# A two-layer transformer kernel: the second attention written out between the weight chunks of its query groups and of the output projection

## Chip, cores and metric

One core of one Trainium2 chip. The metric is the device time of one execution in microseconds (us), lower is better; the kernel before has a median of 2048.22 us in 3 runs (2047.43 to 2049.34).

## What is computed

Two layers on a sequence of 256 tokens with 2048 features, all in float32. Layer 0 has a latent attention (MLA), layer 1 a windowed attention with sinks; each is followed by a feed-forward block with a width-3 convolution. The change lies in layer 1's attention: 32 query heads of 64 features, 4 key/value heads, a window of 128 keys, a bias by distance, and a sink logit per head that enters the softmax's maximum and its sum.

```python
def _swa_sinks(h, rel_bias, w_qkv, b_qkv, sinks, w_o, b_o):
    qkv = h @ w_qkv + b_qkv
    q = qkv[..., :nq] ... * SWA_HEAD_DIM ** -0.5     # 32 heads x 64
    ...
    m, l, acc = _banded_stats(q, k, v, bias, SWA_WINDOW - 1)   # blocks of 128 queries, own and previous block's keys
    m2 = jnp.maximum(m, sink)
    a = jnp.exp(m - m2)
    den = l * a + jnp.exp(sink - m2)
    o = acc * (a / den)[..., None]
    return o.reshape(bsz, t, nq) @ w_o + b_o
```

## The kernel before, in words

**Weights as a stream.** Activations lie transposed in SBUF, features on the 128 partitions and 256 tokens along the row. All weights come as one stream of 682 chunks (128 × 1024 floats, 512 KB), in the order in which they are used; `PH` gives each phase its chunks and its groups of 4 output tiles: a_in, a_q, a_kv, a_out, f0_in, f0_out, b_in (40 chunks, 5 groups), b_out (32 chunks, 4 groups), f1_in, f1_out. Four slots hold chunks in flight. SyncE loads a chunk into `raw` once the slot's last split is done; ScalarE (ACT, L735) rounds it to fp32r as `w_hi`, once TensorE has used the chunk four before; VectorE (DVE, L999) subtracts to get the remainder `w_lo`; TensorE (PE) multiplies. Operands are split in the same way into a high and a low half that lie side by side. For each 128 × 128 block of weights PE makes two matmuls: w_hi with high and low half together (512 columns, L387) and w_lo with the high half (256 columns, L390). One output tile so fills a whole PSUM bank: columns 0 to 255 and 256 to 511 have to be added, and a group of 4 tiles takes 4 of the 8 banks. `token_chunk` (L416 to L418) makes three matmuls of 256 columns instead, with the operand as weights; it gives keys and values by token.

**Leaving PSUM.** `b_half` on ACT (L744) copies the second half of a group's banks to `half_b`; DVE then adds it to the first half (`sum_banks`, L1075, or `add_residual`, L1256 and L1258, for sums into `h`), and frees the banks.

**Second attention.** b_in's first group gives keys and values, the other four the queries (`q_win`). After the last b_in chunk come 16 units of two heads. For each: PE makes the scores (`scores_b`, L676, two heads on the two halves of the rows); DVE adds the bias and takes the maxima (L1189, L1196); ACT takes the exponentials with their sums (L842) and those of the sinks (L846); DVE adds the sinks' to the sums and scales (L1209, L1211, L1218); PE transposes (L551); ACT copies the transposed to SBUF (L854); PE multiplies by the values (`values_b`, L684, L685); ACT and DVE split the result into `op_att` (L966, L1373). GpSimd (POOL) stages keys, values and biases and ACT the queries (L952), because the units run in hardware loops, with fixed places for the operands. Two units are in flight, in eight banks. Only two chunks of b_out are put between the last units (`early_chunk`); else no chunk is multiplied in this stretch. Then b_out goes on group by group, and `residual` adds it to `h`.

All engines run in program order; semaphores between them (`chunk_used`, `lo_ready`, `scores_done`, `maxima_done`, `probs_ready`, `probs_t_copied`, `outputs_done`, `outputs_hi`, `outputs_lo`, `banks_free`) set the order of work.

Of the kernel before, what the change touches and what calls it, by code (L numbers as in the profile page):

```python
# [13 lines left out]
P = 128  # L14
# [56 lines left out]
UNITS_A, UNITS_B = HEADS_A // 2, HEADS_B // 2  # L71

# [77 lines left out]
def build(nc, xt, positions, rel_bias, params, weights, swa_b_v, swa_sinks, c_ident, c_rot, c_invf, c_mask,  # L150
# [37 lines left out]
    sink_exps = new("sink_exps", [P, 2, 4])  # L188
# [58 lines left out]
    q_win = place("q_win", [P, KT, T], F32, rg)  # L249
# [5 lines left out]
    with ctx:  # L255
# [13 lines left out]
        win_bias_in = sem("win_bias_in")  # L269
# [37 lines left out]
        k_both_ready = sem("k_both_ready")  # L307
        nsink_ready = sem("nsink_ready")
        bias_staged = sem("bias_staged")
        q_placed = sem("q_placed")  # L310
# [70 lines left out]
        def _(pe):  # L381
# [252 lines left out]
            def plain_groups(g, n, op, per):  # L634

                for gi in range(2):
                    b0 = banks_of(g + gi)
                    for c in range(per):
                        w_chunk(n + (gi * per + c), op, 2 * c, c == 0, c == per - 1, b0).then_inc(chunk_used, 1)

# [25 lines left out]
            repeat(pe, 0, 2, lambda i: plain_groups(Lin(ph.g0 + 1, 2, i), Lin(ph.c0 + 8, 16, i), op_in, 8))  # L666

            def scores_b(u, bank):
                p = u.mod(2)
                if u.i is None and u.c < 2:  # L670
                    pe.wait_ge(k_both_ready, u.c + 1)
                pe.wait_ge(q_placed, (u + 1).v)
                for hh in range(2):
                    r = slice(64 * hh, 64 * hh + 64)
                    for q0, keys, o in ((0, P, 0), (P, T, P)):
                        z = mm(ps[:, bank + hh, o:o + keys], st_qb[r, p, q0:q0 + P], st_k[r, p, 0:keys],  # L676
                               start=True, stop=True)
                return z

            def values_b(u, bank):  # L680
                p = u.mod(2)
                for hh in range(2):
                    r = slice(64 * hh, 64 * hh + 64)
                    mm(ps[r, bank, 0:T], st_vb[:, p, 0, :], probs_t[p][:, hh, 0:T], start=True, stop=False)  # L684
                    z = mm(ps[r, bank, P:T], st_vb[:, p, 1, :], probs_t[p][:, hh, T:384], start=False, stop=True)  # L685
                return z

            attention(UNITS_A, UNITS_B, scores_b, values_b, attention_banks(PH["b_out"]), ph,
                      early_chunk(PH["b_out"], 2, UNITS_A))
            groups(PH["b_out"], op_att, KT, att_wait(UNITS_A + UNITS_B), start=EARLY)  # L690
# [33 lines left out]
        def _(act):  # L724
# [12 lines left out]
            def b_half(g, last_chunk, tiles=4, bias=None):  # L737

                act.wait_ge(chunk_used, (last_chunk + 1).v)
                if g.i is not None or g.c >= 1:  # L740
                    act.wait_ge(banks_free, g.v)
                b0 = 4 * g.mod(2)
                if bias is None:
                    f(half_b[:, 0:tiles, :], ps[:, b0:b0 + tiles, T:2 * T], ACT.Copy).then_inc(b_copied, 1)  # L744
                    return
                for j in range(tiles):
                    z = f(half_b[:, j, :], ps[:, b0 + j, T:2 * T], ACT.Identity, bias=bias(j))
                z.then_inc(b_copied, 1)
# [86 lines left out]
            def attention(u0, units, banks, sinks, out_high, place_q=None):  # L835
                def exps(u):
# [7 lines left out]
                    if sinks:  # L844
                        for hh in range(2):
                            z = f(sink_exps[:, p, 2 * hh:2 * hh + 2], neg_max[:, p, 2 * hh:2 * hh + 2], ACT.Exp,  # L846
                                  bias=sinkc[:, sl(u.times(2) + hh, 1)])
# [13 lines left out]
                def step(u, ahead=True):  # L861
                    if u.i is not None or u.c >= 2:
                        o_high(u - 2)
                    if ahead:
                        exps(u + 1)
                    if place_q and (u.i is not None or u.c < units - 3):
                        place_q(u + 3)
                    pt_copy(u)
                exps(Lin(0))
                if place_q:  # L870
                    place_q(Lin(2))
# [10 lines left out]
            attention(0, UNITS_A, banks, False,  # L882
# [6 lines left out]
            def residual(ph, kts, k0, bias=None):  # L889
# [3 lines left out]
                def body(i, t=0):  # L893
                    for j in range(2 * per):
                        split(Lin(ph.c0 + AHEAD + j + 2 * per * t, 2 * per, i))
                        gi, at = divmod(j, per)
                        if at == per - 5:
                            b_half(Lin(ph.g0 + gi + 2 * t, 2, i), Lin(ph.c0 + (gi + 1) * per - 1 + 2 * per * t, 2 * per, i),
                                   bias=bias and (lambda m: par[:, sl(Lin(bias + 4 * gi + m, 8, i), 1)]))
                        if at == per - 3 and k0 is not None:  # L900
                            op_high(Lin(k0 + gi, 2, i), op_in[:, sl(Lin(4 * gi, 8, i), 4), 0, :])
                if k0 is not None:
# [35 lines left out]
            def b_body(i):  # L938
                for j in range(16):
                    split(Lin(ph.c0 + AHEAD + SLOTS + j, 16, i))  # L940
                    if j in (7, 15):
                        b_half(Lin(ph.g0 + (j + 1) // 8, 2, i), Lin(ph.c0 + 8 + j, 16, i))
            repeat(act, 0, 2, b_body)
            banks = attention_banks(PH["b_out"])

            def place_q(u):

                if u.i is not None or u.c >= 2:
                    act.wait_ge(scores_done, (u + UNITS_A - 1).v)
# [39 lines left out]
        def _(dve):  # L989
# [144 lines left out]
            def q_group(k, cols, last=False):  # L1134
                dve.wait_ge(b_copied, (k + (ph.g0 + 1)).v)
# [510 lines left out]
```

## Time and profile before

| | |
|---|---|
| median of 3 runs | 2048.22 us |
| profiled execution | 2049.23 us, its span 2047.4 us, mean granted TensorE clock 0.994 |
| busy: PE, PEld, DVE, ACT, POOL | 97%, 86%, 71%, 50%, 9% of the span |
| HBM read | 362.85 MB |

The span runs from the first to the last instruction. Matmuls are pipelined: the time of one holds its way through the array, so that two which follow each other overlap in the rows, and the distance of their starts (the pitch) is what one costs.

### The profile page before, as it was taken

The page shows a single profiled execution, that of the slowest core. Times are in us where ns is not written, and L with a number is a line of the kernel's source. Part 1 is how long each engine was busy: PE and PEld are TensorE (multiplying, and loading weights), DVE is VectorE, ACT ScalarE, POOL GpSimd, SP SyncE. Part 2 cuts the span into 40 slices and gives each one's busy share as a digit, 9 for nine tenths or more (in the row PEclk, how much of TensorE's full clock was granted, in tenths as well). Part 3 has the DMA queues.
Part 4 walks back from the last instruction along what each step waited for, and adds up shares of the span by engine and source line. Part 5 has one row for each costly group of instructions (what it writes and reads, how often), then busy time and mean ns, then how long its engine had stood idle before and what let it go on. Part 6 is the DMA issues. An engine that isn't in the chain of part 4 may idle for free.

```text
span 2047.4 us, 33736 instructions
## 1 busy us (share of the span) xinstructions
PE 1988.8 (97%) x11624; PEld 1750.6 (86%) x11624; DVE 1452.0 (71%) x1988; ACT 1014.0 (50%) x1227; POOL 194.4 (9%) x258
## 2 busy tenths in 40 slices
PE   5999999999999999999999789999999999999998
PEld 5789888888888888888898568888888888888887
DVE  7776588778778877654566767887887787755554
ACT  4456445555554554434344775555545555534343
POOL 4202130000000000110120222200000000001110
PEclk9999999999999999999999899999999999999999
DMA  6458455555555555556576215555555655555553
GB/s 209 135 188 205 152 187 175 190 201 184 192 192 180 184 195 196 187 182 202 188 248 211 88 51 187 188 182 198 185 177 190 202 184 192 191 192 187 193 187 113
DMA packets 103009, 372.25 MB, mean 182 GB/s; under 512 B 11451, under 2 KB 12028, under 8 KB 102940
## 3 DMA queue, kind: packets, MB, share of 16 engines
q1 hardware_dynamic: 100316, 360.45, 52.6%
q0 software_dynamic: 2624, 10.83, 2.1%
q8 instruction: 50, 0.82, 0.2%
q14 instruction: 19, 0.16, 0.0%
HBM read 362.85 MB, written 8.39 MB: 181 GB/s over the span
## 4 chain that ended last, share of the span: by engine, by line
PE 90%; DVE 3%; issue 1%; ACT 0%; DVEq 0%; ACTq 0%
PE ps L387 57%; PE ps L390 30%; DVE scores_sb L1189 1%; DVE probs L1218 1%; PE ps L418 1%; PE ps L417 1%; PE ps L416 1%; PE ps L551 0%; PE ps L598 0%; DVE w_lo L999 0%; PE ps L589 0%; PE ps L591 0%; DVE q_nope L1137 0%; PE ps L676 0%; PE ps L600 0%
## 5 line engine op out<-in xcount | busy, mean ns | idle before, releaser
L999 DVE TENSOR_TENSOR w_lo<-raw,w_hi 128x1024 fp32r<-128x1024 f32 (+1 forms) x682 | 830.6, 1232 | 516.3 <-ACT w_hi L735 493.6
L387 PE MATMUL ps<-op_in,w_hi 128*128 128x512 f32 x3248 | 1120.0, 392 | 20.5 <-DVE w_lo L999 18.9
L735 ACT ACTIVATE w_hi<-raw 128x1024 fp32r<-128x1024 f32 (+1 forms) x682 | 715.5, 1055 | 830.0 <-PE ps L390 673.1
L390 PE MATMUL ps<-op_in,w_lo 128*128 128x256 f32 x3248 | 884.3, 282 | 0.0
L387 PEld LDWEIGHTS ps<-op_in,w_hi 128*128 128x128 f32 x3248 | 598.6, 188 | 135.2 <-issue 18.6
L390 PEld LDWEIGHTS ps<-op_in,w_lo 128*128 128x128 f32 x3248 | 615.8, 190 | 17.0
L387 PE MATMUL ps<-op_ffn,w_hi 128*128 128x512 f32 x1408 | 486.2, 390 | 0.0
L390 PE MATMUL ps<-op_ffn,w_lo 128*128 128x256 f32 x1408 | 391.7, 282 | 0.0
L387 PEld LDWEIGHTS ps<-op_ffn,w_hi 128*128 128x128 f32 x1408 | 262.2, 188 | 53.0
L390 PEld LDWEIGHTS ps<-op_ffn,w_lo 128*128 128x128 f32 x1408 | 266.0, 189 | 2.7
L1408 POOL TENSOR_TENSOR cg<-h 128x1024 f32 (+1 forms) x15 | 43.5, 2898 | 1499.9 <-DVE h L1258 1499.9
L387 PE MATMUL ps<-op_att,w_hi 128*128 128x512 f32 x512 | 176.3, 392 | 2.5 <-issue 2.5
L390 PE MATMUL ps<-op_att,w_lo 128*128 128x256 f32 x512 | 139.0, 282 | 0.0
L387 PEld LDWEIGHTS ps<-op_att,w_hi 128*128 128x128 f32 x512 | 94.0, 188 | 20.8 <-issue 3.2
L390 PEld LDWEIGHTS ps<-op_att,w_lo 128*128 128x128 f32 x512 | 96.7, 189 | 2.6
L1298 DVE SCALAR_TENSOR_TENSOR cv<-up,par,cv 128x256 f32<-128x256 f32 x176 | 73.6, 480 | 6.5 <-DVE cv L1293 3.3
L1298 DVE SCALAR_TENSOR_TENSOR cg<-up,par,cg 128x256 f32<-128x256 f32 x176 | 73.6, 480 | 6.6 <-DVE cg L1293 3.4
L744 ACT ACTIVATE half_b<-ps 128x1024 f32<-128x1024 f32 (+2 forms) x72 | 68.1, 946 | 10.0 <-PE ps L387 10.0
L753 ACT ACTIVATE op_ffn<-cv 128x1024 f32 x22 | 23.4, 1066 | 93.0 <-DVE cv L1323 93.0
L1411 POOL TENSOR_TENSOR sqa<-sqa,cg 128x256 f32<-128x256 f32 x60 | 62.8, 1046 | 4.7
L387 PE MATMUL ps<-op_lat,w_hi 128*128 128x512 f32 x160 | 57.4, 403 | 0.0
L1081 DVE TENSOR_TENSOR up<-up,inv_rms 128x1024 f32<-128x1024 f32 x44 | 53.9, 1225 | 1.5
(178 smaller groups left out, 1233.6 us busy)
## 6 DMA issues: line engine op xcount, KB each, us to landing
raw<-weights SPq DMA_DIRECT2D x666, 512.0 KB, 3.8
raw<-weights SPq DMA_DIRECT2D x16, 384.0 KB, 3.0
bias_rows<-brow POOLq DMA_DIRECT2D x1, 6144.0 KB, 36.2
win_bias<-bias_rows POOLq DMA_DIRECT2D x4, 1024.0 KB, 8.8
h<-xt SPq DMA_DIRECT2D x4, 512.0 KB, 7.0
y<-yt SPq DMA_DIRECT2D x4, 512.0 KB, 3.6
par<-params SPq DMA_DIRECT2D x1, 352.0 KB, 9.7
mask<-c_mask POOLq DMA_DIRECT2D x1, 192.0 KB, 3.7
```

What stands on the lines that cost most here:

```text
L387: return mm(ps[:, bank, 0:2 * T], whi, op, start=start, stop=stop)
L390: return mm(ps[:, bank, 0:T], wlo, op[:, 0, :], start=False, stop=False)
L416: mm(o, hi, wcols(w_hi[s], k), start=first and k == 0, stop=False)
L417: mm(o, hi, wcols(w_lo[s], k), start=False, stop=False)
L735: f(w_hi[s][:, 0:cols], raw[s][:, 0:cols], ACT.Copy).then_inc(hi_ready, 1)
L744: f(half_b[:, 0:tiles, :], ps[:, b0:b0 + tiles, T:2 * T], ACT.Copy).then_inc(b_copied, 1)
L753: f(dst, cv[:, :, :], ACT.Copy).then_inc(operand_hi, 1)
L999: v.tensor_tensor(w_lo[s][:, 0:cols], raw[s][:, 0:cols], w_hi[s][:, 0:cols].bitcast(F32), ALU.subtract).then_inc(lo_ready, 1)
L1081: return v.tensor_tensor(dst, dst, spread(r[:, :], tiles), ALU.mult)
L1298: z = v.scalar_tensor_tensor(dst[:, m, :], up[:, m, tap:T + tap], col(tile0 + (w + tap * CT + m)), dst[:, m, :], ALU.mult, ALU.add)
L1408: done(g_.tensor_tensor(tmp, src, src, ALU.mult))
L1411: z = g_.tensor_tensor(acc[:, :], acc[:, :], tmp[:, j, :], ALU.add)
```

## The change

The second attention is written out, one unit after the other with constants, in between the chunks.

- On PE, chunks of the query groups 2 to 4 and 16 chunks of b_out (tiles 0 to 7; their order in the stream is `OUT_EARLY`) stand between the steps: chunk, transposes of u, chunk, values of u, scores of u+2. There is one set of score banks (0, 1) and one of transposes and values (2, 3).
- These 48 chunks and the first query group are "narrow": three matmuls of 256 columns (w_hi·high, w_lo·high, w_hi·low) that sum in place, two tiles to a bank, so that a group needs two banks and no second half. (32 chunks of queries, 16 of b_out.)
- DVE: `queries` makes a group's queries from the two banks; `q_win` holds two groups. The sink is written as one more column of the scores' rows and goes through the exponential and its sum; the addition of `sink_exps` and its two exponentials go.
- Nothing is staged: GpSimd's copies and ACT's `place_q` go.
- `b_half` goes from all residuals (a_out, f0_out, b_out, f1_out): DVE adds both halves straight from PSUM. b_out's bias is added there.

```diff
+OUT_EARLY = [(0, c) for c in range(6)] + [(1, c) for c in range(6)] + [(0, 6), (0, 7), (1, 6), (1, 7)]
+Q0 = PH["b_in"].c0 + 16
...
+            def narrow_chunk(n, op, kt0, first, last, bank):
+
+                s = n % SLOTS
+                pe.wait_ge(lo_ready, n + 1)
+                for j in range(4):
+                    o = ps[:, bank + j // 2, j % 2 * T:(j % 2 + 1) * T]
+                    for k in range(2):
+                        w = slice(k * COLS + j * P, k * COLS + (j + 1) * P)
+                        mm(o, w_hi[s][:, w], op[:, kt0 + k, 0, :], start=first and k == 0 and j % 2 == 0, stop=False)
+                        mm(o, w_lo[s][:, w], op[:, kt0 + k, 0, :], start=False, stop=False)
+                        z = mm(o, w_hi[s][:, w], op[:, kt0 + k, 1, :], start=False, stop=last and k == 1 and j % 2 == 1)
+                z.then_inc(chunk_used, 1)
...
+            def scores_b_of(u):
+
+                if u == 0:
+                    pe.wait_ge(k_both_ready, KV_B)
+                if u % 4 == 0:
+                    pe.wait_ge(q_win_ready, u // 4 + 1)
+                if u >= 1:
+                    pe.wait_ge(maxima_done, UNITS_A + u)
...
+            def turn_p_b(u):
+
+                pe.wait_ge(probs_ready, UNITS_A + u + 1)
+                if u >= 1:
+                    pe.wait_ge(outputs_lo, UNITS_A + u)
...
+            for u in range(UNITS_B):
+                chunk(4 + 2 * u)
+                turn_p_b(u)
+                chunk(5 + 2 * u)
+                values_b_of(u)
+                if u + 2 < UNITS_B:
+                    scores_b_of(u + 2)
...
+            for u in range(UNITS_B):
+                split(Lin(Q0 + 7 + 2 * u))
+                if u >= 1:
+                    o_high_b(u - 1)
+                if u + 1 < UNITS_B:
+                    exps_b(u + 1)
+                pt_copy_b(u)
+                split(Lin(Q0 + 8 + 2 * u))
...
-                v.tensor_tensor(hh, hh, half_b[:, :, :], ALU.add).then_inc(banks_free, 1)
+                v.tensor_tensor(hh, hh, ps[:, b0:b0 + 4, T:2 * T], ALU.add).then_inc(banks_free, 1)
...
+            for u in range(UNITS_B):
+                if u + 1 < UNITS_B:
+                    maxes_b(u + 1)
+                split(Lin(Q0 + 7 + 2 * u))
+                if u >= 1:
+                    low_b(u - 1)
+                if u in (2, 6, 10):
+                    queries(PH["b_in"].g0 + 2 + u // 4, Q0 + 7 + 2 * (u - 2))
+                if u + 1 < UNITS_B:
+                    normal_b(u + 1)
+                split(Lin(Q0 + 8 + 2 * u))
```

The second of these loops is ACT's, the third DVE's. How the instructions stand, PE first. Before, in the loop of the attention (scores of a unit, transposes, values of the unit before, nothing else):

```order
L676 MATMUL ps<-st_k,st_qb 128x128 [waits q_placed]
L676 MATMUL ps<-st_k,st_qb 128x256
L676 MATMUL ps<-st_k,st_qb 128x128
L676 MATMUL ps<-st_k,st_qb 128x256
L551 MATMUL ps<-ident,probs_81 128x128 [waits probs_t_copied,probs_ready]
L551 MATMUL ps<-ident,probs_81 128x128 x5
L559 REGISTER_ALU [waits values_staged,probs_t_copied]
L684 MATMUL ps<-probs_t_84,st_vb 64x256 [waits outputs_lo]
L685 MATMUL ps<-probs_t_84,st_vb 64x128
```

After the change, a late unit (L728 transposes, L740 values, L717 scores, L679 to L681 a narrow chunk, 24 matmuls of which three stand here):

```order
L728 MATMUL ps<-ident,probs_b_117 128x128 [waits outputs_lo,probs_ready]
L728 MATMUL ps<-ident,probs_b_117 128x128 x5
L679 MATMUL ps<-op_att,w_hi_56 128x256 [waits lo_ready,outputs_lo]
L680 MATMUL ps<-op_att,w_lo_60 128x256
L681 MATMUL ps<-op_att,w_hi_56 128x256
...
L740 MATMUL ps<-probs_tb_119,cv 64x256 [waits probs_t_copied]
L740 MATMUL ps<-probs_tb_119,cv 64x256
L740 MATMUL ps<-probs_tb_119,cv 64x128 x2
L717 MATMUL ps<-k_both,q_win 128x128 [waits maxima_done]
L717 MATMUL ps<-k_both,q_win 128x128
L717 MATMUL ps<-k_both,q_win 128x256 x2
L679 MATMUL ps<-op_att,w_hi_53 128x256 [waits lo_ready,outputs_lo,banks_free]
```

A chunk now stands on either side of the transposes, and these wait for `outputs_lo` of the unit before as well. DVE before, from a unit's negative maxima to the low half of an older unit's output:

```order
L1196 SCALAR_TENSOR_TENSOR neg_max<-ri,nsink 128x4
L1209 TENSOR_TENSOR exp_sums<-exp_sums,sink_exps 128x4 [waits exps_done]
L135 REGISTER_ALU
L1211 RECIPROCAL ri<-exp_sums 128x4 [waits dve_done]
L135 REGISTER_ALU
L1218 TENSOR_SCALAR probs_81<-scores_sb,ri 128x128 [waits probs_transposed,dve_done]
L1218 TENSOR_SCALAR probs_81<-scores_sb,ri 128x256
L1218 TENSOR_SCALAR probs_81<-scores_sb,ri 128x128
L1218 TENSOR_SCALAR probs_81<-scores_sb,ri 128x256
L1373 ISA [waits outputs_hi]
L1373 REGISTER_ALU
L1373 TENSOR_TENSOR op_att<-ps,op_att 128x256
```

DVE after, from the copy of the sinks (L1477) on; L1084 is a chunk's split, L1504 the low half (`low_b`), L1472 the next unit's sums of scores and bias:

```order
L1477 COPY scores_b<-sinkc 128x2x2
L1481 SCALAR_TENSOR_TENSOR neg_max<-ri,nsink 128x4 [waits dve_done]
L1084 TENSOR_TENSOR w_lo_58<-raw_50,w_hi_54 128x1024 [waits hi_ready]
L1504 TENSOR_TENSOR op_att<-ps,op_att 128x256 [waits outputs_hi]
L1490 RECIPROCAL ri<-exp_sums 128x4 [waits exps_done]
L1497 TENSOR_SCALAR probs_b_118<-scores_b,ri 128x128 [waits probs_transposed,dve_done]
L1497 TENSOR_SCALAR probs_b_118<-scores_b,ri 128x256
L1497 TENSOR_SCALAR probs_b_118<-scores_b,ri 128x128
L1497 TENSOR_SCALAR probs_b_118<-scores_b,ri 128x256
L1084 TENSOR_TENSOR w_lo_59<-raw_51,w_hi_55 128x1024 [waits hi_ready]
L1472 ISA scores_b,ri<-ps,win_bias 128x128 [waits probs_ready,scores_done]
```

A split now stands between the maxima and the low half, and another behind the scaling.

## Rows read from the trace of the kernel before

**Rows 1.** The page: busy time and share of the span; PE's busy tenths in 40 slices

```profile
PE 1988.8 (97%) x11624; PEld 1750.6 (86%) x11624; DVE 1452.0 (71%) x1988; ACT 1014.0 (50%) x1227; POOL 194.4 (9%) x258
PE   5999999999999999999999789999999999999998
```

**Rows 2.** Windows: length, PE, PEld, DVE, ACT, POOL busy, granted clock, DMA, GB/s

```profile
1150.00:1160.00 10.00, 5.26 (x25) 3.50 (x25) 7.57 (x46) 9.05 (x33) 3.51 (x12) 0.67 0.00 2
1180.00:1190.00 10.00, 7.68 (x66) 5.02 (x66) 9.14 (x50) 10.00 (x40) 5.32 (x21) 1.00 0.00 0
```

**Rows 3.** Timeline of PE, end of b_in: start, length, instruction, idle before

```profile
1143.43 0.39 PE L387 MATMUL ps<-op_in,w_hi 128*128 128x512 f32 x1
1147.13 2.97 PE L676 MATMUL ps<-st_k,st_qb 64*128 64x128 f32 x16 [3.32 <-ACT st_qb L952]
```

**Rows 4.** Timeline of PE and DVE, end of the attention and early chunks

```profile
1208.29 0.82 PE L551 MATMUL ps<-ident,probs 128*128 128x128 f32 x6
1209.04 0.66 PE L684 MATMUL ps<-probs_t,st_vb 128*64 128x256 f32 x4
...
1209.84 0.50 PE L387 MATMUL ps<-op_att,w_hi 128*128 128x512 f32 x1
...
1212.62 0.28 PE L390 MATMUL ps<-op_att,w_lo 128*128 128x256 f32 x1
1212.82 0.66 PE L684 MATMUL ps<-probs_t,st_vb 128*64 128x256 f32 x4
...
1214.17 0.42 DVE L1373 TENSOR_TENSOR op_att<-ps,op_att 128x256 fp32r<-128x256 f32 x1 [3.36 <-ACT op_att L966]
1214.70 0.48 PE L387 MATMUL ps<-op_att,w_hi 128*128 128x512 f32 x1 [1.00 <-issue]
```

**Rows 5.** Timeline of PE, steady part: transposes, scores, transposes 11 units on

```profile
1162.92 0.87 PE L551 MATMUL ps<-ident,probs 128*128 128x128 f32 x6 [0.18 <-DVE probs L1218]
...
1164.89 0.93 PE L676 MATMUL ps<-st_k,st_qb 64*128 64x128 f32 x8 [0.30 <-ACT st_qb L952]
...
1200.81 0.88 PE L551 MATMUL ps<-ident,probs 128*128 128x128 f32 x6 [0.52 <-DVE probs L1218]
```

**Rows 6.** Timeline of PE: token chunk's 12 matmuls, then plain pairs 80 apart

```profile
1038.44 0.28 PE L416 MATMUL ps<-w_hi,op_in 128*128 128x256 f32 x1
...
1039.86 0.39 PE L387 MATMUL ps<-op_in,w_hi 128*128 128x512 f32 x1
...
1103.41 0.39 PE L387 MATMUL ps<-op_in,w_hi 128*128 128x512 f32 x1
...
1131.17 0.39 PE L387 MATMUL ps<-op_in,w_hi 128*128 128x512 f32 x1
```

**Rows 7.** Timeline of DVE: split, queries' scaling, probs, maxima, probs again

```profile
1142.17 1.23 DVE L999 TENSOR_TENSOR w_lo<-raw,w_hi 128x1024 fp32r<-128x1024 f32 x1 [1.55 <-ACT w_hi L735]
...
1149.17 1.14 DVE L1365 TENSOR_SCALAR q_win<-cg,par 128x256 f32 x4 [0.26 <-DVE cg L1081]
...
1189.34 1.59 DVE L1218 TENSOR_SCALAR probs<-scores_sb,ri 128x128 f32<-128x128 f32 x4
...
1201.02 0.28 DVE L1189 CUSTOM_DVE_ANT_0 scores_sb<-ps,st_b 128x128 f32<-128x128 f32 x1
...
1202.24 0.16 DVE L1196 SCALAR_TENSOR_TENSOR neg_max<-ri,nsink 128x4 f32<-128x4 f32 x1
...
1202.72 1.01 DVE L1218 TENSOR_SCALAR probs<-scores_sb,ri 128x128 f32<-128x128 f32 x4
```

**Rows 8.** Timeline of ACT: first exponential, sinks', transposed copy of a unit

```profile
1189.55 0.41 ACT L842 ACTIVATE scores_sb<-scores_sb,neg_max 128x128 f32<-128x128 f32 x1
...
1191.31 0.49 ACT L846 ACTIVATE sink_exps<-neg_max,sinkc 128x2 f32<-128x2 f32 x2
...
1191.99 0.81 ACT L854 ACTIVATE probs_t<-ps 128x768 f32<-128x768 f32 x1
```

**Rows 9.** The chain at the end, and DVE's last sums in the timeline

```profile
2031.38 1.03 ACT half_b L744
...
2032.44 1.22 DVE L1256 TENSOR_TENSOR h<-h,ps 128x1024 f32<-128x1024 f32 x1 [9.78 <-ACT half_b L744]
```

More of the change, by code:

```diff
@@ L71, with b_count, b_banks @@
 UNITS_A, UNITS_B = HEADS_A // 2, HEADS_B // 2
+def b_count(g):
+    first = g.c if g.i is None else g.c + g.k
+    n = g + 1 - sum(PH[p].ng for p in ("a_out", "f0_out", "b_out") if first > PH[p].g0)
+    return n - (PH["b_in"].ng - 1) if first > PH["b_in"].g0 else n
+OUT_EARLY = [(0, c) for c in range(6)] + [(1, c) for c in range(6)] + [(0, 6), (0, 7), (1, 6), (1, 7)]
+Q0 = PH["b_in"].c0 + 16
+def b_banks(g):
+    return {PH["b_in"].g0 + 1: 0, PH["b_in"].g0 + 2: 4, PH["b_in"].g0 + 3: 6, PH["b_in"].g0 + 4: 4,
+            PH["b_out"].g0: 6, PH["b_out"].g0 + 1: 4}[g]
 def attention_banks(ph_out):
@@ L680, in values_b @@
[L680 to L689, printed above, removed]
@@ L742, in b_half @@
                 b0 = 4 * g.mod(2)
[L743 to L748, printed above, removed]
+                f(half_b[:, 0:tiles, :], ps[:, b0:b0 + tiles, T:2 * T], ACT.Copy).then_inc(b_copied, 1)
             def op_high(k, dst):
@@ L832, in _, with attention @@
             kv_group(Lin(7), False)
-            def attention(u0, units, banks, sinks, out_high, place_q=None):
+            def attention(u0, units, banks, out_high):
                 def exps(u):
@@ L970, in _ @@
+            split(Lin(Q0 + 45))
+            op_high(Lin(OP0["b_out"] + 1), op_in[:, 4:8, 0, :])
+            split(Lin(Q0 + 46))
+            split(Lin(Q0 + 47))
+            residual(PH["b_out"], KT, OP0["b_out"], second=True)
             norm_root(5, inv_rms[:, :], 4 - 4 * (PH["f1_in"].g0 % 2), D)
@@ new lines, in low_b @@
+            def low_b(u):
+                dve.wait_ge(outputs_hi, UNITS_A + u + 1)
+                v.tensor_tensor(op_att[:, u, 1, :], ps[:, 2, 0:T], op_att[:, u, 0, :].bitcast(F32),
+                                ALU.subtract).then_inc(outputs_lo, 1)
+            for n in range(Q0 - 4, Q0 + 4):
+                split(Lin(n))
+            queries(PH["b_in"].g0 + 1, Q0 - 1)
+            split(Lin(Q0 + 4))
+            split(Lin(Q0 + 5))
+            maxes_b(0)
+            split(Lin(Q0 + 6))
@@ new lines, in _, with narrow_residual @@
+            low_b(UNITS_B - 1)
+            split(Lin(Q0 + 40))
+            split(Lin(Q0 + 41))
+            def narrow_residual(gi, last_chunk):
+                g = PH["b_out"].g0 + gi
+                dve.wait_ge(chunk_used, last_chunk + 1)
+                for m in range(4):
+                    hm = h[:, 4 * gi + m, :]
+                    z = v.scalar_tensor_tensor(hm, ps[:, b_banks(g) + m // 2, m % 2 * T:(m % 2 + 1) * T],
+                                               col(Lin(PC_BO + 4 * gi + m)), hm, ALU.add, ALU.add)
+                z.then_inc(banks_free, 1)
+                dve.wait_ge(banks_free, g + 1)
@@ L1378, in _ @@
+            operand(Lin(OP0["b_out"] + 1), op_in, Lin(4))
+            split(Lin(Q0 + 47))
+            residual(PH["b_out"], KT, OP0["b_out"], PC_FFN + KT, bias=PC_BO, second=True)
             inverse(5, [inv_rms[:, :]])
```

331 lines of the change are left out of this document (190 added, 141 removed).

## The prediction, made before the changed kernel ran

> **What bounds the kernel now.** I read the page first: TensorE (PE) is busy for 97% of the span, VectorE (DVE) for 71%, and PE's line over the 40 slices has one dip, a 7 and an 8 at slices 23 and 24 [rows 1]. So almost everything is already hidden behind the matmuls, and a change can win only where PE is not fed. Next the windows: at that dip, the ten microseconds from 1150 have 5.26 of 10 busy at a granted clock of 0.67, those from 1180 have 7.68 with the DMA queues at 0 GB/s [rows 2]. That is the second attention, which streams no weights. The timeline of PE gives its two edges: the last b_in matmul starts at 1143.43, the third chunk of b_out (the first with no attention work behind it) at 1214.70 [rows 3, 4]. A chunk's last and next matmul lie 0.23 us apart, so the stretch is 1214.70 − 1143.66 = **71.0 us**. Inside it: 3.32 us of PE idle before the first scores [rows 3], then a steady part in which the transposes of one unit follow those of the one before by (1200.81 − 1162.92)/11 = 3.44 us [rows 5], and 1.00 us at the end, before the third chunk [rows 4].
>
> **Prices on PE.** A chunk of weights today is 8 pairs of a 512- and a 256-column matmul: 80 pairs from 1103.41 to 1131.17, 0.347 us a pair, 2.78 us a chunk [rows 6]. The new narrow chunk is 24 matmuls of 256 columns. The token chunks of b_in are just that: 12 of them from 1038.44 to 1039.86, 0.118 us each [rows 6], so a narrow chunk takes 24 × 0.118 = 2.84 us. An attention unit: the transposes start 0.75 us before the values (1208.29, 1209.04), the values 0.80 before the next work (1209.84) [rows 4]. The scores show as 0.93 us [rows 5]; such a time holds the drain of the last matmul, which overlaps the next work: a lone 256-column matmul shows as 0.28 us at a pitch of 0.12 [rows 6]. Here the next full-array work starts some 0.1 before the end, so I take 0.85. The first weight matmul behind such work takes 0.50 us instead of 0.39 [rows 3, 4], 0.11 more, twice a unit once chunks stand in between; a values step behind a chunk starts 0.20 behind its last matmul (1212.62, 1212.82) where 0.12 is the pitch, 0.08 more. Together 0.75 + 0.80 + 0.85 + 0.22 + 0.08 = 2.70 us a unit.
>
> **The change, part by part.**
>
> *Removed: the stretch in which PE waits.* 71.0 us go, and what comes back is the work in them: 16 units × 2.70 = 43.2 us, and two chunks of 2.78, 5.6 us. If nothing else happened: −22.2.
>
> *Narrow chunks.* 32 of the queries' and 16 of the output projection's chunks become narrow: 48 × (2.84 − 2.78) = **+2.9 us**. The Trainium skill (TensorE: Matmul & The Clock Gate, Back-to-back issue gap) gives 262 cycles for 256 columns and 518 for 512, by which three narrow matmuls would cost 786 cycles against 780 for the pair, an estimate of 0.02 us a chunk and 1 us in all; the rows show three times that, and I keep the rows.
>
> *Switches between small and full-array work.* The rows just priced hold them, 0.08 to 0.11 us each. From above, a switch may cost the time that a lone matmul takes from start to end, 0.28 us [rows 6], 0.2 more than I count: 16 × 2 × 0.2 = 6.4 us, the far bound. The Trainium skill (TensorEngine Tiling, Key Properties) says that changing the tiling mode drains the engine, which speaks against mixing 64-row and 64-column work with chunks; by that rule with a whole drain at each switch the sum would be 6 us worse, by the rows it is not.
>
> *The new chain from unit to unit.* PE runs chunk, transposes(u), chunk, values(u), scores(u+2), and each step waits in order. Let scores(u+1) start at 0. They are seen at 0.93. DVE then does the sums of maxes_b(u+1): 1.22 us from the first to the negative maximum today (1201.02, 1202.24) [rows 7], about 0.1 to the next operation, plus a copy of the sinks, for which 4 small elements per row cost like the other small ones, some 0.1: to 2.4. Next in DVE's order is the split of a chunk, 1.23 us [rows 7], to 3.6, and only then low_b(u−1), 0.42 us, to 4.0, after which PE starts 0.1 later (1214.17 + 0.42, then 1214.70) [rows 4]. The transposes of u write the bank that low_b reads, and wait for it until 4.1. But PE is done with scores and chunk at 0.85 + 0.11 + 2.84 = 3.8. So it **waits 0.3 to 0.4 us in each unit**; I take 0.38. Units 1 to 14 have it (unit 0 has no predecessor, in unit 15 no maxima stand ahead): 14 × 0.38 = 5.3 us. Bounds: nothing, if DVE is 0.4 quicker (GpSimd's copies, which run beside it today, are gone: the four probs operations take 1.59 us in one unit and 1.01 in another [rows 7], and I put the difference on them); 0.9 if the sink copy costs a whole 0.3 and the split 0.2 more.
>
> *The rest of a unit hides.* ACT gets the maxima at 2.5; its four exponentials take 1.8 (1189.55 to 1191.31, the sinks' own two are gone) to 4.3, the transposed copy 0.8 from 5.0 (0.93 behind the transposes' start) to 5.8 [rows 8]; PE needs it behind its second chunk at 4.1 + 0.75 + 2.95 = 7.8: 2 us of slack. The second split of the unit: ACT 5.9 to 6.9, DVE to 8.2, before scores(u+2) are seen at 9.6. A unit is 8.7 us long; In three units queries() stands behind low_b, 1.22 + 0.3 + 1.14 us [rows 7, 9]: 4.0 + 2.7, then the reciprocal and the four probs operations (0.2 + 1.01) and the split (1.23) end at 9.1, still before 9.6. Weights: a chunk's split ends over 9 us before its matmuls, and its load is queued a chunk round earlier.
>
> *At the front,* counted from the end of the first query group: scores(1) need the maxima of unit 0. DVE has a split (to 2.3), queries() (to 5.0), a split (to 6.2), one more that waits for ACT and the second chunk (2 × 2.84, +1.1, +1.23: to 8.1) and the sums (to 9.6), PE three chunks and scores(0), to 9.4: +0.3. *At the back,* counted from the end of values(15): low_b(15) is done at some 2.0 (ACT's split to 0.4 and its copy, DVE's split to 1.6 and the 0.4), and chunk 37, which waits for it, comes at 2.9 anyway; the split of chunk 41 ends at 5.8 + 1.1 + 1.23 = 8.2, the four sums of narrow_residual by 10, and the first plain group, which waits for them, begins at 4 × 2.84 + 0.1 = 11.5. Nothing.
>
> *Residuals without the half_b copy.* In a_out, f0_out, f1_out and the rest of b_out ACT's copy of the second half goes (1 us each, hidden: PE has no idle there), and DVE reads both halves from PSUM at 1.22 us as before [rows 9]. Only the last one is on the path: ACT's copy from 2031.38, DVE's sum from 2032.44 [rows 9]: **−1.1 us**.
>
> *GpSimd* loses its staging; nobody waits for it any more.
>
> **Sum.** −71.0 + 43.2 + 5.6 + 2.9 + 5.3 + 0.3 − 1.1 = **−14.8 us**. That is worked out in the profiled execution (2049.2 us, span 2047.4), 1.0 us above the median of the runs shown, 2048.2. I put it on the median: **2033.4 us**.
>
> **Rivals.**
> 1. *The wait for low_b does not appear* (DVE 0.4 us quicker, or PE's unit longer): −14.8 − 5.3 = −20.1, 2028.1. For it: 0.38 is a small difference of two sums of 4 us. Against: each of the durations has its row. 0.2.
> 2. *The wait is larger*, 0.9 a unit, or the drains cost 6 us: −14.8 + 7 = −8, 2040. For it: no row shows the sink copy or a chunk behind scores. 0.17.
> 3. *Slower: ACT's order.* The transposed copy of u stands behind the exponentials of u+1. It has 2 us. If maxima or exponentials come over 2 us later than above, values(u) wait, and every further microsecond is paid in each of 14 units; over 1.1 us beyond that point eats the 14.8 and the kernel gets slower, about 2050 at 1.2 beyond. Against: DVE and ACT each have under 6.2 us of work in 8.7. 0.03.
> 4. *No change*: the chunks moved between the units only spread the same waits. It would need PE to stay idle some 20 us, which DVE's and ACT's load does not give. 0.03.
> The forecast (−11.5 to −18): 0.57.
>
> **Range.** From no wait and somewhat cheaper scores (−22, 2026.5) to the large wait (−9, 2039). Faster, by more than 0.2% or 4.1 us (about what a measurement of this kernel can tell from no change): 0.94; within: 0.03; slower: 0.03.
>
> **What would show it.** In the new profile: no window of the second attention under 9 in 10 for PE, the granted clock at 1.00 and the DMA queues moving throughout; 24 matmuls in 2.84 us; one idle of PE per unit, ahead of the transposes, of about 0.4 us and released by DVE's subtraction into op_att; units 8.7 us apart; no ACT row between the last matmul and the last sum into h. I am wrong if the idle sits ahead of the values (ACT's order), ahead of a chunk (splits late), or if scores and values take clearly more than 0.85 and 0.80 us.

## The result, and the profile after

| | before | after |
|---|---|---|
| median, lowest and highest (4 runs each, same chip) | 2047.82 (2047.03 to 2049.34) | 2060.33 (2058.21 to 2062.77) |
| span of the profiled execution | 2047.4 | 2061.0 |

The ratio of after to before is 1.0057 [1.0042, 1.0072]: the changed kernel is 0.6% slower, where 2033.4 us and a gain were forecast. The page and the windows of the changed kernel, in the same columns as [rows 1] and [rows 2]:

```profile
PE 2018.2 (98%) x12008; PEld 1763.8 (86%) x12008; DVE 1445.3 (70%) x1978; ACT 982.4 (48%) x1145; POOL 167.4 (8%) x168
PE   5999999999999999999999999999999999999998
```

```profile
1150.00:1160.00 10.00, 9.91 (x86) 8.62 (x83) 6.19 (x25) 5.29 (x14) 0.00 (x0) 1.00 0.42 145
1180.00:1190.00 10.00, 9.91 (x85) 8.96 (x84) 6.14 (x22) 6.27 (x14) 0.00 (x0) 1.00 0.44 145
```

The dip is gone, the granted clock is 1.00, the weights flow: the change did what it says. And yet the time rose. So it must have gone somewhere that nobody was looking at. I cut the span at two places that both kernels have: the first matmul of the first query group behind the token chunks, and the first plain chunk of b_out behind its 16th. Timeline of PE, in before, in after, and in the first experiment (e1, below). In before's second row the second of two matmuls is meant, which starts at 1253.41 + 0.62 − 0.39 = 1253.64.

```profile
1054.83 0.39 PE L387 MATMUL ps<-op_in,w_hi 128*128 128x512 f32 x1
...
1253.41 0.62 PE L387 MATMUL ps<-op_att,w_hi 128*128 128x512 f32 x2
```

```profile
1071.62 0.28 PE L679 MATMUL ps<-op_in,w_hi 128*128 128x256 f32 x1
...
1253.82 0.40 PE L398 MATMUL ps<-op_att,w_hi 128*128 128x512 f32 x1
```

```profile
1054.81 0.28 PE L680 MATMUL ps<-op_in,w_hi 128*128 128x256 f32 x1
...
1234.70 0.39 PE L399 MATMUL ps<-op_att,w_hi 128*128 128x512 f32 x1
```

| us | before | after | after − before | e1 | e1 − before |
|---|---|---|---|---|---|
| up to the first query group | 1054.8 | 1071.6 | **+16.8** | 1054.8 | 0.0 |
| query groups, attention, 16 chunks of b_out | 198.8 | 182.2 | −16.6 | 179.9 | −18.9 |
| the rest | 793.8 | 807.2 | **+13.4** | 794.1 | +0.3 |

The stretch that was rewritten is 16.6 us shorter. The loss is 30.2 us in the two stretches in which the change only drops the residuals' copies and adds b_out's bias elsewhere. Both are made of pairs of matmuls; here is one place of them, the timeline of PE in before and then in after:

```profile
1700.31 0.39 PE L387 MATMUL ps<-op_in,w_hi 128*128 128x512 f32 x1
1700.54 0.28 PE L390 MATMUL ps<-op_in,w_lo 128*128 128x256 f32 x1
1700.66 0.39 PE L387 MATMUL ps<-op_in,w_hi 128*128 128x512 f32 x1
1700.89 0.28 PE L390 MATMUL ps<-op_in,w_lo 128*128 128x256 f32 x1
1701.01 0.39 PE L387 MATMUL ps<-op_in,w_hi 128*128 128x512 f32 x1
```

```profile
1700.08 0.40 PE L398 MATMUL ps<-op_in,w_hi 128*128 128x512 f32 x1
1700.32 0.28 PE L401 MATMUL ps<-op_in,w_lo 128*128 128x256 f32 x1
1700.43 0.40 PE L398 MATMUL ps<-op_in,w_hi 128*128 128x512 f32 x1
1700.67 0.28 PE L401 MATMUL ps<-op_in,w_lo 128*128 128x256 f32 x1
1700.79 0.40 PE L398 MATMUL ps<-op_in,w_hi 128*128 128x512 f32 x1
```

From a 512-column matmul to the next start it is 0.23, 0.23 before and 0.24, 0.24 after; two pairs take 0.70 and 0.71. Two digits hardly show it; the mean over all starts in the trace that no wait and no other work put off does: 228.5 + 118.3 = 346.8 ns a pair before, 235.9 + 116.8 = 352.7 after. The page's groups of costly instructions have it too, in the mean length of one (before, then after):

```profile
L387 PE MATMUL ps<-op_in,w_hi 128*128 128x512 f32 x3248 | 1120.0, 392 | 20.5 <-DVE w_lo L999 18.9
L387 PE MATMUL ps<-op_ffn,w_hi 128*128 128x512 f32 x1408 | 486.2, 390 | 0.0
```

```profile
L398 PE MATMUL ps<-op_in,w_hi 128*128 128x512 f32 x2992 | 1047.8, 399 | 21.9 <-DVE w_lo L1084 20.3
L398 PE MATMUL ps<-op_ffn,w_hi 128*128 128x512 f32 x1408 | 495.3, 399 | 0.0
```

The whole kernel has 2992 + 1408 + 384 + 160 = 4944 such pairs left (op_in, op_ffn, op_att, op_lat): 4944 × 5.9 ns = 29.2 us. By the trace 2704 of them stand in the first stretch (16.0 us) and 2240 in the third (13.2 us). Same instruction, same shape, same clock: what differs is where the operands lie. The diff deletes a 32-byte tile that stood ahead of them:

```python
    exp_sums = new("exp_sums", [P, 2, 4])
-    sink_exps = new("sink_exps", [P, 2, 4])
    ri = new("ri", [P, 2, 4])
...
    fence = new("fence", [P, 12])
...
    ra = region(KT * 2 * T * 4)      # op_in
...
    rg = region(FT * 2 * T * 4)      # op_ffn; op_att and op_lat lie in it
```

Tiles are placed one behind the other, each rounded up to 32 bytes a partition. Between the weights' slots and `op_in` most sizes are multiples of 128; the others (`up`, `rs_col`, `eps`, `neg_max`, `exp_sums`, `sink_exps`, `ri` with 32 over each, `fence` with 64) sum to 288, 32 over a multiple of 128. Without `sink_exps` they sum to 256, and operands and weights lie at the same place within 128 bytes.

### The profile page after: what moved, and what is told of

Its sections match the earlier page's. It is cut to its first block, busy times and chain, and to the rows that moved or that the text cites. A ratio compares the mean times of both kernels' runs of the same rounds, so it can differ in the third digit from the quotient of the medians.

```text
span 2061.0 us, 33818 instructions
## 1 busy us (share of the span) xinstructions
PE 2018.2 (98%) x12008; PEld 1763.8 (86%) x12008; DVE 1445.3 (70%) x1978; ACT 982.4 (48%) x1145; POOL 167.4 (8%) x168
## 4 chain that ended last, share of the span: by engine, by line
PE 93%; DVE 2%; issue 0%; ACT 0%; DVEq 0%; ACTq 0%
PE ps L398 54%; PE ps L401 27%; PE ps L679 2%; PE ps L680 2%; PE ps L681 2%; PE ps L717 1%; PE ps L728 1%; PE ps L740 1%; DVE w_lo L1084 1%; PE ps L428 1%; PE ps L429 1%; PE ps L427 1%; DVE cv L1099 0%; PE ps L609 0%; PE ps L600 0%
## 5 line engine op out<-in xcount | busy, mean ns | idle before, releaser
L1084 DVE TENSOR_TENSOR w_lo<-raw,w_hi 128x1024 fp32r<-128x1024 f32 (+1 forms) x682 | 838.7, 1238 | 526.5 <-ACT w_hi L810 504.0
L398 PE MATMUL ps<-op_in,w_hi 128*128 128x512 f32 x2992 | 1047.8, 399 | 21.9 <-DVE w_lo L1084 20.3
L398 PEld LDWEIGHTS ps<-op_in,w_hi 128*128 128x128 f32 x2992 | 551.2, 189 | 145.3 <-issue 18.5
L401 PEld LDWEIGHTS ps<-op_in,w_lo 128*128 128x128 f32 x2992 | 566.5, 189 | 16.8
L398 PE MATMUL ps<-op_ffn,w_hi 128*128 128x512 f32 x1408 | 495.3, 399 | 0.0
L398 PE MATMUL ps<-op_att,w_hi 128*128 128x512 f32 x384 | 134.5, 399 | 2.5 <-issue 1.5
L401 PE MATMUL ps<-op_att,w_lo 128*128 128x256 f32 x384 | 103.8, 281 | 0.0
L398 PEld LDWEIGHTS ps<-op_att,w_hi 128*128 128x128 f32 x384 | 70.6, 188 | 18.5 <-issue 1.6
L679 PE MATMUL ps<-op_in,w_hi 128*128 128x256 f32 x256 | 74.3, 290 | 0.0
L401 PEld LDWEIGHTS ps<-op_att,w_lo 128*128 128x128 f32 x384 | 72.5, 189 | 2.1
L681 PE MATMUL ps<-op_in,w_hi 128*128 128x256 f32 x256 | 72.3, 282 | 0.0
```

The costliest lines, as they stand in the source:

```text
L398: return mm(ps[:, bank, 0:2 * T], whi, op, start=start, stop=stop)
L401: return mm(ps[:, bank, 0:T], wlo, op[:, 0, :], start=False, stop=False)
L679: mm(o, w_hi[s][:, w], op[:, kt0 + k, 0, :], start=first and k == 0 and j % 2 == 0, stop=False)
L681: z = mm(o, w_hi[s][:, w], op[:, kt0 + k, 1, :], start=False, stop=last and k == 1 and j % 2 == 1)
L1084: v.tensor_tensor(w_lo[s][:, 0:cols], raw[s][:, 0:cols], w_hi[s][:, 0:cols].bitcast(F32), ALU.subtract).then_inc(lo_ready, 1)
```

## The experiments

"Distance" below is the operand's place minus that of `w_hi`, modulo 128 bytes; "pitch" the mean start to start of a 512-column and a 256-column matmul of a pair in the trace. Counting modulo 128 is a way of writing it: in the changed kernel the operands lie a multiple of 512 bytes past the weights, and e1, e4 and e8 add 32, 64 and 96. No run adds 128 and nothing else. Where a run has no interval, it is a single time.

**e1_pad32: give the 32 bytes back, and nothing else.**

```diff
     fence = new("fence", [P, 12])
+    region(32)
```

> The changed kernel with 32 unused bytes in front of the operands (op_in, op_ffn, op_att, op_lat), which puts them back to 32 bytes past a multiple of 64, as before the change; nothing else differs. Theory A (the removal of sink_exps moved the operands by 32 bytes, and TensorE's 512-column matmuls read them more slowly there): their pitch falls from 236 to 228 ns, and the time falls by some 4944 pairs x 5.9 ns = 29 us, to 2031 us. Theory B (something else in the changed kernel, its longer program or the sums straight from PSUM, slows the matmuls): pitch 236 ns, 2060 us.

2030.83 us (2030.49 to 2031.67), ratio to before 0.9914 [0.9897, 0.9930]. The pitch is 228.5 and 118.3 again, and the table above shows the outer stretches back at before's lengths. 29.5 us under the changed kernel, from 32 unused bytes. The stretch between has no pairs, and it gained as well: its 1152 narrow matmuls have a mean pitch of 119.7 ns in after and 116.9 in e1, which makes 3.2 us. The table has 2.3 of them (182.2, 179.9), mostly because PE's wait ahead of the transposes grew from 0.25 to 0.30 us in 14 units.

**e2_before_shift: the kernel before, with `sink_exps` allocated last.** Not one instruction differs from before.

```diff
-    sink_exps = new("sink_exps", [P, 2, 4])
...
     op_ffn = place("op_ffn", [P, FT, 2, T], F32R, rg)
...
+    sink_exps = new("sink_exps", [P, 2, 4])
```

> The kernel before with its sink_exps (32 bytes) placed behind all other tiles, so that the operands move down by 32 bytes to a multiple of 64; the instructions are the same. Theory A: the pitch of the 512-column matmuls rises from 228 to 236 ns, 2048 + 5328 pairs x 5.9 ns = 2079 us. Theory B: no change, 2048 us.

2079.52 us (2077.02 to 2082.54), ratio 1.0154 [1.0137, 1.0171]. 5328 pairs × 5.9 ns are 31.4 us, measured 30.9 over the 2048.66 that before took on the same chip. Its page, to be held against the first row of before's two above:

```profile
L387 PE MATMUL ps<-op_in,w_hi 128*128 128x512 f32 x3248 | 1136.6, 399 | 21.2 <-DVE w_lo L999 19.6
```

So the cause is shown from both sides. The next five runs ask what about the place matters.

**e3_rg32: 32 bytes behind `op_in` alone, ahead of `op_ffn`, `op_att`, `op_lat`.**

```diff
+    region(32)
     rg = region(FT * 2 * T * 4)
```

> The changed kernel with the 32 unused bytes behind op_in and in front of op_ffn, op_att and op_lat: op_in stays at a multiple of 64. Theory A, each matmul by its own operand's address: L398 with op_in keeps 236 ns, with op_ffn, op_att and op_lat it goes to 228; 1952 pairs x 5.9 ns = 11.5 us less than the changed kernel, 2049 us. If only the distance of all tiles to the weights or the whole layout counted, all or none would change.

2048.22 us, 12.1 under the changed kernel where 1952 pairs × 5.9 ns are 11.5, and the page parts the operands:

```profile
L399 PE MATMUL ps<-op_in,w_hi 128*128 128x512 f32 x2992 | 1047.5, 399 | 20.9 <-DVE w_lo L1085 19.4
L399 PE MATMUL ps<-op_ffn,w_hi 128*128 128x512 f32 x1408 | 486.2, 390 | 0.0
```

Each matmul is slow or fast by its own operand's place: those from `op_in` stayed at 399, those from `op_ffn` went to 390.

**e4_pad64 and e8_pad96: 64 and 96 bytes instead of 32.**

```diff
     fence = new("fence", [P, 12])
+    region(64)      # e8: region(96)
```

> The changed kernel with 64 unused bytes in front of the operands. If the place within 64 bytes is what counts, as slow as the changed kernel (pitch 236 ns, 2060 us); if any other place than the changed one is fast, or if it goes by 128 bytes, 228 ns and 2031 us.

> The changed kernel with 96 unused bytes in front of the operands: weights at 64, operands at 32 (mod 128 bytes), the one place in steps of 32 not yet seen. If 32 past a multiple of 64 is good whatever the rest: 228 ns and 2031 us, as with 32 bytes of padding. If it goes by 128 bytes, some other pitch between 228 and 236 ns.

2040.44 us (230.3 and 118.7 ns) and 2049.13 us (232.0 and 118.0). It isn't one good and one bad case: four places, four pitches.

**e5_all32 and e6_weights32: is it the place of a tile, or how two lie to each other?** e5 moves weights and operands together by 32 bytes, e6 the weights by 32 and the operands by 64.

```diff
+    region(32)
     raw = [new(f"raw{s}", [P, CH]) for s in range(SLOTS)]
...
     fence = new("fence", [P, 12])
+    region(32)      # e6 only
```

> The changed kernel with 32 unused bytes in front of all tiles: the weight slots (until now at 64 past a multiple of 128 bytes) and the operands (in the changed kernel at 64 too) both move to 96. Theory A1, only the operands' own place counts: they stand where the kernel before has them, pitch of L398's matmul 228 ns, 2031 us. Theory A2, the distance between the weights' place and the operands' counts (both at the same place within 128 bytes is bad): pitch 236 ns, 2060 us.

> The changed kernel with 32 unused bytes in front of all tiles and 32 more in front of the operands: weights at 96, operands at 0 (mod 128 bytes). A1: as in the run with 64 bytes of padding, where the operands stood at 0: 230 ns and 2040 us. A2: distance 32, as in the kernel before: 228 ns and 2031 us.

e5, distance 0 at other places: 2061.3 us and 235.9, 116.8 ns, as after. e6, distance 32 at other places: 2030.73 us and 228.5, 118.3, as e1. In these two runs the distance counts and the place by itself doesn't.

**e7_low_first: the wait ahead of the transposes.** Back to the forecast's own terms. In the changed kernel a unit looks like this on PE (the last of a chunk's 24 matmuls, transposes, the first of a chunk; then values, scores, the next chunk and the next unit's transposes):

```profile
1161.87 0.28 PE L681 MATMUL ps<-op_in,w_hi 128*128 128x256 f32 x1
1162.24 0.85 PE L728 MATMUL ps<-ident,probs_b 128*128 128x128 f32 x6
1162.84 0.36 PE L679 MATMUL ps<-op_in,w_hi 128*128 128x256 f32 x1
...
1165.68 0.28 PE L681 MATMUL ps<-op_in,w_hi 128*128 128x256 f32 x1
1165.89 0.87 PE L740 MATMUL ps<-probs_tb,cv 128*64 128x256 f32 x8
1166.69 0.93 PE L717 MATMUL ps<-k_both,q_win 64*128 64x128 f32 x8
1167.54 0.38 PE L679 MATMUL ps<-op_in,w_hi 128*128 128x256 f32 x1
...
1170.39 0.28 PE L681 MATMUL ps<-op_in,w_hi 128*128 128x256 f32 x1
1170.76 0.85 PE L728 MATMUL ps<-ident,probs_b 128*128 128x128 f32 x6
```

The last matmul of a chunk and the transposes lie 0.37 us apart, where the matmul's own pitch is 0.12: 0.25 us of waiting. And DVE in the same unit, from the first sum of scores and bias:

```profile
1159.14 0.29 DVE L1472 CUSTOM_DVE_ANT_0 scores_b<-ps,win_bias 128x128 f32<-128x128 f32 x1 [1.52 <-PE ps L717]
...
1160.26 0.17 DVE L1477 COPY scores_b<-sinkc 128x4 f32<-128x4 f32 x1
1160.46 0.17 DVE L1481 SCALAR_TENSOR_TENSOR neg_max<-ri,nsink 128x4 f32<-128x4 f32 x1
1160.54 1.22 DVE L1084 TENSOR_TENSOR w_lo<-raw,w_hi 128x1024 fp32r<-128x1024 f32 x1
1161.68 0.42 DVE L1504 TENSOR_TENSOR op_att<-ps,op_att 128x256 fp32r<-128x256 f32 x1
```

`low_b` ends at 1162.10, the transposes start at 1162.24. e7 is e1 with `low_b` ahead of the split:

```diff
                 if u + 1 < UNITS_B:
                     maxes_b(u + 1)
-                split(Lin(Q0 + 7 + 2 * u))
                 if u >= 1:
                     low_b(u - 1)
+                split(Lin(Q0 + 7 + 2 * u))
```

> The changed kernel with 32 bytes of padding, and in DVE's order low_b(u-1) ahead of the chunk's split instead of behind it. Theory: PE's wait ahead of the transposes, 0.30 us in each of units 1 to 14 in the run with padding alone, comes from DVE reaching low_b 1.2 us too late; it goes, a unit is 8.15 instead of 8.45 us long, and the time falls by 4.2 us, from 2030.8 to 2026.6. Rival: the wait only moves (to the probabilities or the split), the unit stays at 8.45 us, 2031 us.

2025.45 us (2024.77 to 2026.91), ratio 0.9888 [0.9871, 0.9904]: 5.4 under e1 where 4.2 were expected. The last matmul and the transposes are a pitch apart now, and a unit is 8.11 us long (8.45 in e1, 8.52 in after):

```profile
1101.34 0.29 PE L682 MATMUL ps<-op_in,w_hi 128*128 128x256 f32 x1
1101.46 0.82 PE L729 MATMUL ps<-ident,probs_b 128*128 128x128 f32 x6
...
1109.57 0.81 PE L729 MATMUL ps<-ident,probs_b 128*128 128x128 f32 x6
```

**e9_tail: the wait behind the attention.** After has one wait that before lacks, in b_out's first plain group; then DVE from the split ahead of it, and GpSimd:

```profile
1269.11 0.51 PE L398 MATMUL ps<-op_att,w_hi 128*128 128x512 f32 x1 [1.00 <-DVE w_lo L1084]
```

```profile
1253.51 4.43 DVE L1099 TENSOR_SCALAR cv<-h,par 128x256 f32<-128x256 f32 x4
1257.86 1.21 DVE L1084 TENSOR_TENSOR w_lo<-raw,w_hi 128x1024 fp32r<-128x1024 f32 x1
...
1261.82 2.92 DVE L1084 TENSOR_TENSOR w_lo<-raw,w_hi 128x1024 fp32r<-128x1024 f32 x1
1264.66 3.26 DVE L1099 TENSOR_SCALAR cv<-h,par 128x256 f32<-128x256 f32 x4
```

```profile
1252.41 2.93 POOL L1587 TENSOR_TENSOR cg<-h 128x1024 f32 x1 [150.65 <-DVE h L1537]
1255.42 4.25 POOL L1590 TENSOR_TENSOR sqa<-sqa,cg 128x256 f32<-128x256 f32 x4
```

The four gains of an operand take 4.43 and 3.26 us where four TENSOR_SCALARs of the same size took 1.14 in [rows 7], and a split 2.92 instead of 1.22, each beside GpSimd's squares (2.93 us for one, then four additions). Not every such overlap costs DVE something: the split at 1257.86 takes 1.21 us beside GpSimd. Narrow windows show which of the two is the long one, first a gain that starts behind a square, then the last addition, which starts behind that split:

```profile
1253.51 1.98 DVE L1099 TENSOR_SCALAR cv<-h,par 128x256 f32<-128x256 f32 x1
1257.87 1.80 POOL L1590 TENSOR_TENSOR sqa<-sqa,cg 128x256 f32<-128x256 f32 x1
```

A lone gain takes 0.35 us at the kernel's end, and the addition before this one 0.74. The split of 2.92 us starts at 1261.82, behind a square that runs from 1260.84 to 1263.66. So in these cases the operation that starts second is the long one. The other three gains of that operand start within 0.01 us of an addition and take 0.89 to 0.90 us each. e9 is e7 with the splits of chunks that PE needs soon put ahead of the gains and operands of the second tile group (DVE, and ACT's likewise):

```diff
             split(Lin(Q0 + 44))
-            operand_gains(1)
             split(Lin(Q0 + 45))
+            operand_gains(1)
             split(Lin(Q0 + 46))
-            operand(Lin(OP0["b_out"] + 1), op_in, Lin(4))
             split(Lin(Q0 + 47))
+            operand(Lin(OP0["b_out"] + 1), op_in, Lin(4))
```

> The kernel of the run with low_b first, and in b_out's first plain group the split of chunk 45 ahead of the gains of the second operand, the splits of chunks 46 and 47 ahead of that operand's two halves (on DVE and ACT). Theory: PE's single wait of 1.29 us for a split there comes from DVE's four gains operations, which take 3 to 4.5 us instead of 1.1 while GpSimd squares; with the splits ahead of them it goes: 2025.5 - 1.3 = 2024.2 us. Rival: later splits or operands come late in turn and PE waits as long somewhere else, 2025.5 us.

2023.85 us (2022.18 to 2025.26), ratio 0.9876 [0.9859, 0.9892]. The wait (1.29 us in e1 and e7) is gone from the trace, and the window from 1071 to 1234 has PE busy for all of its 163 us. The step of 1.6 us is within the spread of the two runs' times; that the wait is gone is shown, its price in the time only likely.

**e10_lo96, e11_lo32, e12_lo32_timed, e13_lo64: the two halves of the weights apart.** Until here `w_lo` lay as `w_hi` does. These four are e9 with unused bytes between them, to find whose distance sets which pitch.

```diff
     w_hi = [new(f"w_hi{s}", [P, CH], F32R) for s in range(SLOTS)]
+    region(32)      # e11, e12; e10: 96; e13: 64
     w_lo = [new(f"w_lo{s}", [P, CH], F32R) for s in range(SLOTS)]
+    region(32)      # e10 only; e13: 64
...
     fence = new("fence", [P, 12])
-    region(32)      # out in e10, e11, e12; stays in e13
```

> As the run before this one, with operands and w_hi at the same place within 128 bytes (distance 0, as in the changed kernel) and w_lo moved so that the operands lie 32 past it. Theory N (a matmul is slowed by the load of the weights for the next one, so the distance to the other half of the weights counts): the 512-column matmul, during which w_lo is loaded, 228 ns, the 256-column one, during which the next w_hi is loaded, 116.8 ns: 4944 x 1.5 ns = 7 us less, 2017 us. Theory O (a matmul's own weights count): 236 and 118.3 ns, 2024 + 4944 x 7.5 ns = 2061 us.

> The reverse: operands 32 past w_hi, as in the kernel before, and at the same place as w_lo. Theory N: 236 and 118.3 ns, 2061 us. Theory O: 228 and 116.8 ns, 2017 us.

> The reordered kernel with the operands 32 past w_hi, as in the kernel before, and w_lo 64 further on, so that the operands lie 96 past it (mod 128 bytes). Theory D (what counts is that w_hi and w_lo don't lie at the same place, as in the two runs with w_lo moved): the 512-column matmul at 226.5 to 227 ns, as there. Theory E (each distance has its own price, 96 being the second worst where both had it, 232 ns): between 228.5 and 232 ns.

> The kernel with the operands 32 past w_hi and at the same place as w_lo, once more and timed, since its single execution (2019.2 us) was the shortest: if the shorter pitch of the pairs (344.6 instead of 346.8 ns) is what shortened it, 4 to 8 us less than the reordered kernel's 2023.9, 2016 to 2020 us; if the single execution was luck, 2023 us.

| run | distance to w_hi, w_lo | pitch 512, 256 columns (ns) | time (us) |
|---|---|---|---|
| e5 (as after) | 0, 0 | 235.9, 116.8 | 2061.3 |
| e6 (as e1, before) | 32, 32 | 228.5, 118.3 | 2030.7 |
| e4 | 64, 64 | 230.3, 118.7 | 2040.4 |
| e8 | 96, 96 | 232.0, 118.0 | 2049.1 |
| e10 | 0, 32 | 226.8, 119.9 | 2025.08, ratio 0.9881 [0.9864, 0.9897] |
| e12 (e11 single: 2019.18) | 32, 0 | 226.7, 118.0 | **2015.56**, ratio 0.9840 [0.9827, 0.9854] |
| e13 | 32, 96 | 236.6, 116.6 | 2053.7 |

The times of the last three are to be held against e9's 2023.85. None of the ideas recorded ahead of e10, e11 and e13 held. A rule by the matmul's own weights fails: at distance 32 to w_hi the wide matmul takes 228.5 ns (e1) or 226.7 (e12), by where w_lo lies. A rule by the other half alone fails too: at distance 0 to w_lo it takes 235.9 (after) or 226.7 (e12). So both places count at once, and seven points don't give the rule. The rows of e10 and e13 carry less: in bytes added to the changed kernel's distances they are 128 and 32, and 160 and 96, and that 128 counts as 0 is assumed, not shown. e12, the best version of the study, was found this way rather than derived; it has the fastest pair, 344.7 ns, and 4944 × 2.1 ns = 10.4 us less than e9 were to be had by it, 8.3 measured. The narrow matmuls went the other way, from a mean of 116.8 to 117.9 ns: 1152 × 1.1 ns = 1.3 us of the difference. The page of e12:

```profile
L399 PE MATMUL ps<-op_in,w_hi 128*128 128x512 f32 x2992 | 1026.4, 391 | 20.6 <-DVE w_lo L1085 19.0
```

## Why the prediction was wrong

**The step that failed** is one that the sum makes without saying: "If nothing else happened: −22.2", and then terms for the attention, its chunks, the residuals and the tail alone. Every matmul outside was carried over at its price before. 4944 pairs at [rows 6]'s 0.347 us were held for a constant of the instruction; it depends on the layout, and the diff's line `-    sink_exps = new(...)` changed it to 0.353. That is +29.2 us, twice the whole forecast gain; e1 takes 29.5 us back with 32 bytes, and e2 makes the old kernel 30.9 us slower by the same move. None of the four rivals had it; the one for "slower" had ACT's order as its mechanism, and that didn't occur.

**The forecast of the change itself** holds once the layout is put back: e1 takes 2030.83, forecast 2033.4, inside the range of 2026.5 to 2039. Two misses of opposite sign stand behind that, −5.2 us in the stretch and +1.29 at the back; with either alone it would have stayed inside. By its terms:

- *The stretch*: −71.0 + 43.2 + 5.6 + 2.9 + 5.3 + 0.3 = −13.7 forecast; −18.9 in e1. The transposes cost 0.60 us up to the next chunk (1162.24, 1162.84), not the 0.75 taken from [rows 4], where values followed them: 16 × 0.15 = 2.4. The wait for `low_b` is 0.30 in e1, not 0.38: 1.1. A narrow chunk takes 2.81, not 2.84: 48 × 0.03 = 1.4; this too is the layout, since in after it is 24 × 119.7 ns = 2.87. Together 4.9 of the 5.2. Values are at 0.80 (1165.89, 1166.69) and scores at 0.85 (1166.69, 1167.54), as forecast.
- *The chain from unit to unit*: right in place, in its releaser and in the engine order behind it. One idle a unit, ahead of the transposes, behind `low_b`; taking the split from between ended it (e7). A unit is 8.52 us long in after and 8.45 in e1, where 8.7 was forecast.
- *Switches*: the far bound of 6 us didn't come. A chunk's first matmul costs 0.23 us to the next one's start behind the scores instead of 0.12, and 0.20 behind the transposes, which use the full array as the chunk does. So not all of the extra is a matter of the array's shape.
- *ACT's order and everything else in a unit*: hidden, as forecast. PE has no other idle in the unit.
- *At the back, "Nothing"*: wrong by 1.00 us in after, 1.29 in e1. The forecast followed DVE up to the start of the first plain group and stopped there. The gains and operands that DVE has to do between that group's splits stand in no sum, and by [rows 7]'s 1.14 us for four such operations they would have looked small. The trace of before had the higher price for this very operation:

```profile
1238.05 4.43 DVE L1014 TENSOR_SCALAR cv<-h,par 128x256 f32 x4
```

- *Residuals, −1.1*: right. No row of ACT stands between the last matmul and the last sums; DVE starts 8.90 us behind its last work, straight behind PE, and PE's idle that the timeline puts ahead of the final transposes is 0.82 us against 1.88 before. Timeline of the end, one row of before and two of after:

```profile
2034.98 1.09 PE L702 MATMUL ps<-ident,h 128*128 128x128 f32 x8 [1.88 <-DVE h L1258]
...
2046.24 1.22 DVE L1329 TENSOR_TENSOR h<-h,ps 128x1024 f32<-128x1024 f32 x1 [8.90 <-PE ps L398]
2048.77 1.09 PE L777 MATMUL ps<-ident,h 128*128 128x128 f32 x8 [0.82 <-DVE h L1336]
```

The terms close: outside the stretch e1 differs from before by 0.0 + 0.3 us, which are −1.06 for the tail and +1.29 for the wait at the back.

**What stays open.** Why the distance sets the pitch, and after how many bytes it repeats. What the runs fix is that it is by matmul (e3), by distance and not place (e5, e6), and that both halves of the weights enter (e1, e12 and after). The Trainium skill (TensorE: Matmul & The Clock Gate, Step-by-step: what each phase is for) says that the moving operand and the weight load have read ports of their own, so that loading the next weights takes nothing from a running matmul. The page names no price for where the two lie. Between e1 and after that place makes 29.5 us, and whether a port, a memory bank or something else is behind it, no run here shows.

## What to carry to other kernels

When most of the span is one instruction repeated some thousand times, compare its start-to-start time first, to the nanosecond, in stretches that the change doesn't touch; a difference there of 1.7% outweighed everything else here. A deleted or resized small tile moves all that is placed behind it, where tiles are laid one behind the other: keep the distance between moving operands and weights fixed by placing them first or with explicit padding, and try the few distances, since they cost no instruction. Which one is best has to be measured, as these runs give no rule. And price an engine's work by rows in which its neighbours do what they will do at the new place.

## What the hardware showed that I had not expected

- A pair of fp32r matmuls (512 and 256 columns, full clock) takes 344.7 ns (e12) to 353.2 (e13) by the distances of the operand to both halves of the weights, 2.5% from best to worst. On this kernel's 4944 pairs that is 42 us.
- The 256-column pitch moves against the 512-column one in part: 116.6 to 116.8 where the wide one takes 236, 118.0 to 119.9 where it takes 227 to 232. A view of either form alone misjudges the sum. Three matmuls of 256 columns in a row go by the distance too, 119.7 ns in after and 116.9 in e1.
- Four DVE TENSOR_SCALARs of 256 columns take 4.43 us beside GpSimd's squares and 1.14 without. The Trainium skill (SBUF — State Buffer, Who interferes with whom) calls the port pair of DVE and GpSimd an exclusive lock that blocks the second to issue; the rows agree for the gain at 1253.51 and the split at 1261.82, which start behind a square, and for GpSimd's addition of 1.80 us, which starts behind a split. They do not settle the gains of 0.89 us, which start within 0.01 us of GpSimd's additions, and no run here took GpSimd's work away.
